# Another order of columns in the moving operand and the result of the large matmuls

## The chip, the core and the metric

The kernel runs on one core of one Trainium2 chip. The metric is the device time in microseconds of one execution; the runs shown have a median of 3166.25 us. The profiled execution was recorded by the hardware profiler, and its span goes from the first to the last instruction.

## The reference

Two transformer blocks, one after the other, over 256 tokens of width 2048, all in float32. The first mixes an HGRN2 recurrence, dilated window attention and a convolution; the second an mLSTM in chunks and differential attention. Each ends in a feed-forward layer. Cut to what the change touches:

```python
# first block
h = rms_norm(x, mix_norm_pre) * (1 + sc1) + sh1
a_q, a_f, a_i, a_g, b_q, b_k, b_v, c_a, c_g = split_cols(h @ w_in, IN_SPLITS)
gates = sigmoid(h @ w_gate + b_gate)              # 2048 x 6144
merged = gates[0] * (ya @ w_a_out) + gates[1] * (yb @ w_b_out) + gates[2] * (yc @ w_c_out)
x = x + g1 * rms_norm(merged @ w_o, mix_norm_post)
h = rms_norm(x, mlp_norm_pre) * (1 + sc2) + sh2
x = x + g2 * rms_norm(square(relu(h @ w_up)) @ w_down, mlp_norm_post)   # 8192 wide
# second block
p_lat, p_ctx = modulate(rmsnorm(x)) @ w_in_2, modulate(rmsnorm(ctx)) @ w_in_2
...                                               # mLSTM and attention over p_lat, p_ctx
x = x + ga1 * rmsnorm(y_lat, g_post_mix)
x = x + ga2 * rmsnorm(conv_ffn(h_lat, w_up_2, conv_ffn_w, conv_ffn_b, w_down_2), g_post_ffn)  # 2 x 5632 wide
```

## The kernel before, in words

Activations lie with their features on the 128 partitions and the 256 tokens along the partition. A weight matrix is cut into blocks of 2048 rows by 128 columns, laid out as `[128, 16, 128]`; these blocks are the `stream` in HBM, 1 MB each. `SECTIONS` writes their order out by hand: a "G" is a block for a matrix product, an "A" a block of the modulation weights, which VectorE multiplies and sums (`ada_column`, L1755 to L1763). SyncE loads the stream in this order into the four slots of `raw`, each as soon as the block before it in its slot is `taken`.

Precision comes from a split. A number is kept as a rounded high part and a low part, both of type float32r. ScalarE writes the high part of a weight block to `parts[:, b % 2, 0]` (`split_high`, L540), VectorE the low part to `parts[:, b % 2, 1]` (`split_low`, L1782). Activations are split in the same way. The products are high times high, high times low and low times high, so a block of 16 row tiles takes 48 matmuls of 256 columns, and each matmul has a weight load of its own.

Most blocks go through `product`, with pieces made by `features`: first, for each of the 16 row tiles k, the high weights against the high and the low part of the activations (L1041, 32 matmuls), then the low weights against the high part (L1050, 16). `gemm_T` does this for sections `a_f`, `a_q`, `b_k`, `b_q`, `a_g`, the first nine blocks of `gate`, the gates in `merge`, `w_o`, most of `up1` and `up2`, `m_q` and `d_q`. The `down` sections use `gemm_parts`, where the high and low parts of the activations lie side by side (`both`, 512 columns): 16 matmuls of 512 columns (L1077; 11 in `down2`) and as many of 256 columns (L1080), and VectorE adds the halves of the result. Others are made without these two: `branches`, `gate_chunk`, `gemm_two`, `gemm_tokens` (the weights are the moving operand there, in two runs of 128 columns), `features_wide` (512 columns in two runs, from `op_hw`, in `m_k` and `d_k`), and the work within the attention and recurrence stages.

SBUF is allocated by hand. All activation operands are regions of one arena that start at multiples of 512 bytes from one another; `parts` lies behind it, and L191 puts a gap of 16 floats (64 bytes) ahead of it:

```python
raw = sb("raw", [P, SLOTS, KT, P])
sb("parts_gap", [P, 16])
parts = sb("parts", [P, 2, 2, KT, P], F32R)
```

The feed-forward layers go in four quarters: `up1_0`, `down1_0`, `up1_1` and so on; `up2_q` and `down2_q` likewise. The row of stages in time is that of `SECTIONS`. TensorE waits for `hi_ready` (the high part of the block), for `bank_read` (the PSUM bank is free again) and, before the low part, for `taken`. There are two buffers of `parts` and four PSUM banks for results, so a block's split can run at most two blocks ahead.

Of the kernel before, what the change touches and what calls it, by code (L numbers as in the profile page):

```python
# [14 lines left out]
S = 256  # L15
D = 2048
KT = D // P
SLOTS = 4
EARLY_SLOTS, N_EARLY = 8, 48
EPS = 1e-6  # L20
TINY = 1e-30
# [46 lines left out]
def gb(name, i=0):  # L68

    return FIRST[name][1] + i  # L70
# [81 lines left out]
def two_blocks_kernel(nc, stream, x_t, ctx_t, vec_d, const_d, lvl_mask_d, ident_d, rel_bias, c_rows, scratch, x_keep, out_t):  # L152
    with ExitStack() as ctx:
        def sb(name, shape, dt=F32):
            return ctx.enter_context(nc.sbuf_tensor("sb_" + name, shape, dt))
# [33 lines left out]
        arena = sb("arena", [P, ARENA])  # L189
# [3 lines that stand above are left out]
# [172 lines left out]
        def use(n):  # L365

            if n < N_EARLY:
                return n % EARLY_SLOTS, n // EARLY_SLOTS
            return n % SLOTS, N_EARLY // EARLY_SLOTS + (n - N_EARLY) // SLOTS

        def slot_of(slot):

            return raw[:, slot] if slot < SLOTS else early_slots[slot - SLOTS]

        def kt_of(b):
            if b < KT:
                return 2 * C_TILES
            return UP2 if any(gb(f"down2_{q}") <= b < gb(f"down2_{q}") + 16 for q in range(QUARTER)) else KT
# [5 lines left out]
        def scores_bank(unit, c):  # L384

            return (M if unit % 2 == 0 else G)[c]
# [26 lines left out]
        def bank(b):  # L413
            return G[BANK[b]]
# [30 lines left out]
        @block.sync  # L445
        def _(sp):
            kts = [KT] * N_STREAM
            for b, n in enumerate(G_AT):
                kts[n] = kt_of(b)
            context_at = A_AT[127] + SLOTS  # L450

            for n in range(N_STREAM):
                slot, uses = use(n)
                if uses:
                    sp.wait_ge(taken[slot], uses)
                sp.dma_start(slot_of(slot)[:, 0:kts[n], :], stream[n][:, 0:kts[n], :]).then_inc(loaded[slot], 16)
                if n == context_at:
                    sp.wait_ge(x_ready, 5)
                    sp.dma_start(hfc, ctx_t).then_inc(cx_in, 16)
            for c, (k0, k1) in enumerate(CHUNKS):  # L460
                sp.wait_ge(x_ready, 15 + c + 1)
                sp.dma_start(out_t[:, k0:k1, :], xT[:, k0:k1, :]).then_inc(stored, 16)
            sp.wait_ge(stored, 80)
# [16 lines left out]
        def _(act):  # L480
# [50 lines left out]
            def split_high(b):  # L531

                if b >= len(G_AT):
                    return
                slot, uses = use(G_AT[b])
                kt = kt_of(b)
                act.wait_ge(loaded[slot], 16 * (uses + 1))
                if b >= 2:
                    act.wait_ge(hi_used, b - 1)
                act.activation(parts[:, b % 2, 0, 0:kt, :], slot_of(slot)[:, 0:kt, :], ACT.Copy).then_inc(hi_ready, 1)  # L540
# [478 lines left out]
        def _(pe):  # L1019
# [38 lines left out]

            def features(out, op, k0=0, k1=KT, cols=slice(0, S), kw=0):

                return (out, True, [(lambda w, x, k=k: (w[:, kw + k - k0, :], x), op[:, 0, k, cols], op[:, 1, k, cols])
                                    for k in range(k0, k1)])

            def gemm_T(b, op, it=0, dn=0, cols=slice(0, S), kt=KT, waits={}):
                product(b, [features(bank(b)[:, 0:cols.stop - cols.start], op, 0, kt, cols)], it, dn, waits=waits)

            def gemm_parts(b, op, it=0, kt=KT, waits={}):


                slot, uses = use(G_AT[b + it * 4])  # L1070
                pe.wait_ge(hi_ready, b + 1 + it * 4)
                pe.wait_ge(bank_read[BANK[b]], NTH[b] + it)
                for k in range(kt):
                    if k in waits:
                        pe.wait_ge(*waits[k])
                    both = op[:, :, k, :].rearrange("p a s -> p (a s)")
                    pe.matmul(bank(b)[:, :], parts[:, b % 2, 0, k, :], both, start=(k == 0), stop=False, skip_group_check=True)  # L1077
                pe.wait_ge(taken[slot], uses + 1)
                for k in range(kt):
                    ins = pe.matmul(bank(b)[:, 0:S], parts[:, b % 2, 1, k, :], op[:, 0, k, :], start=False, stop=(k == kt - 1),  # L1080
                                    skip_group_check=True)
                    if k == 0:
                        ins.then_inc(hi_used, 1)
                ins.then_inc(block_done, 1)

            def down_round(section, op, it, r, kt=KT, waits={}):
                for j in range(4):
                    gemm_parts(gb(section) + 4 * r + j, op, it, kt, waits if r == j == 0 else {})
# [94 lines left out]
            def ada(a, rows=M[2]):  # L1183


                slot, uses = use(A_AT[a])
                pe.wait_ge(loaded[slot], 16 * (uses + 1))
                for k in range(KT):
                    g = k % 4
                    ins = pe.matmul(rows[32 * g:32 * g + 32, 0:P], cpad[:, k, 32:64], slot_of(slot)[:, k, :],  # L1190
                                    start=(k < 4), stop=(k >= KT - 4), skip_group_check=True)
                ins.then_inc(taken[slot], 1)
# [41 lines left out]
            for n in range(4):  # L1234
                ins = pe.matmul(G[n][:, :], ones[0:1, :], c1_early[0:1, n * 512:(n + 1) * 512], start=True, stop=True)
# [26 lines left out]
            def head_row(h, src):  # L1262


                g, j = divmod(h, 2)
                return pe.matmul(M[0][32 * g:32 * g + 32, 0:S], head_sum[:, 31 - j:63 - j], src, start=(j == 0), stop=(j == 1))
# [48 lines left out]
            for n in range(BESIDE_LEVELS):  # L1315
# [19 lines left out]
                if s in (36, 37):  # L1335
                    for h in (0, 2, 4, 1, 3, 5) if s == 36 else (6, 7):
                        pe.wait_ge(o_sq, h // 2 + 1)
                        ins = head_row(h, fP[:, h, :])
# [34 lines left out]
            for u in range(10):  # L1373
                if u < 8:
                    T, slot = u // 4, u % 4
                    w = P * (T + 1)
                    if u >= 1:
                        pe.wait_ge(qk_read, u)
                    for g in range(3):
                        h = 4 * g + slot  # L1380
                        po = 64 * (h % 2)
                        out = M[0][:, g * S:g * S + w] if g < 2 else M[1][:, 0:w]
                        ins = pe.matmul(out, bq[po:po + 64, h // 2, T * P:(T + 1) * P], bk[po:po + 64, h // 2, 0:w],
                                        start=True, stop=True)
# [5 lines left out]
                if 1 <= u < 9:  # L1390
                    e, T = (u - 1) % 2, (u - 1) // 4
# [3 lines left out]
                    for i, (g, st) in enumerate((g, st) for g in range(3) for st in range(T + 1)):  # L1395
                        ins = pe.matmul(M[2 + i // 4][:, (i % 4) * P:(i % 4 + 1) * P], blog[e][:, g, st * P:(st + 1) * P],
                                        bdg[e], start=True, stop=True)
# [3 lines left out]
                if u >= 2:  # L1401
                    T, slot, e = (u - 2) // 4, (u - 2) % 4, (u - 2) % 2
# [5 lines left out]
                    for i, (g, st) in enumerate(chunk):  # L1408
                        hc = (4 * g + slot) * 64
                        ins = pe.matmul(G[3][po:po + 64, 0:P], bv[:, st, hc:hc + 64], bpt[e][:, i, :],  # L1410
                                        start=(i == 0), stop=(i == len(chunk) - 1))
# [19 lines left out]
            for t in range(EARLY_ROUNDS, 16):  # L1431
                b = gb("merge") + 4 * (t - EARLY_ROUNDS)
# [28 lines left out]
            for k in range(KT):  # L1461
                gemm_parts(gb("down1_3", k), opU1, waits=waits if k == 0 else {})
                if k == 3:
                    norm_folded(sqc, 3)
# [11 lines left out]
            for i in range(2):  # L1476
                b = gb("m_k", i)
# [28 lines left out]
            for d in range(2):  # L1506
                for t in range(2):
                    at = 64 + d * 16 + t * 8
                    ins = pe.matmul(M[1][:, at:at + 8], floor_rows[0:8, d, t * P:(t + 1) * P], ident[0:8, 0:8], start=True, stop=True)
# [102 lines left out]
            for i in range(0, 8, 2):  # L1612
# [6 lines left out]
                for c in range(i, i + 2):  # L1619
                    if c >= 2:  # L1620
                        pe.wait_ge(rope_done, c - 1)
                    for j in range(2):
                        src = dq[:, 2 * c + j, :] if c < 4 else dk[:, 2 * (c - 4) + j, S:512]
                        ins = pe.matmul(M[c % 2][:, j * S:(j + 1) * S], rtab[:, 0:P], src, start=True, stop=True)
# [37 lines left out]
            for u in range(19):  # L1662
                if u < 16:
# [3 lines left out]
                    for c in range(2):  # L1667
                        ins = pe.matmul(scores_bank(u, c)[:, :], dq[64 * c:64 * c + 64, h, T * P:(T + 1) * P], dk[64 * c:64 * c + 64, h, :],
                                        start=True, stop=True)
# [4 lines left out]
                if 2 <= u < 18:  # L1674
                    e = u % 2
# [3 lines left out]
                    for t in range(4):  # L1679
                        ins = pe.transpose(M[2][:, t * P:(t + 1) * P], dpd[e][:, t * P:(t + 1) * P], ident[:, :])  # L1680
# [3 lines left out]
                if u >= 3:  # L1684
                    h, e = (u - 3) // 2, (u - 3) % 2
# [4 lines left out]
                    for t in range(4):  # L1690
                        ins = pe.matmul(M[3][:, 0:P], dv[:, t, h * P:(h + 1) * P], dPT[e][:, t, :], start=(t == 0),
                                        stop=(t == 3))
# [43 lines left out]
            for k in range(KT):  # L1736
                gemm_parts(gb("down2_3", k), opU2, kt=UP2, waits=waits if k == 0 else {})
# [4 lines left out]
        def _(dve):  # L1742
# [23 lines left out]
            def ada_made(a_end):  # L1766


                for a in range(a_end - SLOTS, a_end):
                    slot, uses = use(A_AT[a])  # L1770
# [809 lines left out]
```

## Time and profile before

| | |
|---|---|
| median of the runs | 3166.25 us (3160.32 to 3176.34) |
| profiled execution | 3166.26 us, its span 3164.5 us |
| mean granted TensorE clock | 0.996 |
| busy: TensorE, its weight loads, VectorE, ScalarE | 3095.9, 2919.9, 2369.1, 1336.6 us |
| read from HBM | 712.41 MB |

Busy time is the union of an engine's instructions. A matmul's length includes its way through the array and overlaps the next one's, so the distance from one start to the next is the time that a matmul takes in a row of many; a busy time divided by a count comes near it. A weight load (PEld) overlaps the matmuls. A window's row has its length, then the busy time (and in brackets the count of the instructions that lie in it or across its edges) of TensorE, weight loads, VectorE, ScalarE and GpSimd, then the granted TensorE clock, the busy share of the DMA engines and GB/s.

### The profile page before, as it was taken

How to read it: one execution, taken by the hardware profiler on the slowest of the kernel's cores; microseconds unless marked ns; L12 is line 12 of the kernel's file. 1: busy time of each engine (PE TensorE's matmuls, PEld its weight loads, DVE VectorE, ACT ScalarE, POOL GpSimd, SP SyncE). 2: the span in 40 equal slices, each digit the busy share in tenths (PEclk: the TensorE clock that was granted, in tenths of full speed). 3: DMA queues.
4: the chain of work that ended last, by engine and by line, in shares of the span. 5: the costliest groups of instructions: out<-in, count | busy, mean ns of one | idle time of the engine just before them, and what ended most of it. 6: DMA issues, size and time to landing. Idle time of an engine off the chain costs nothing.

```text
span 3164.5 us, 55394 instructions
## 1 busy us (share of the span) xinstructions
PE 3095.9 (98%) x23974; PEld 2919.9 (92%) x23974; DVE 2369.1 (75%) x2843; ACT 1336.6 (42%) x1459; POOL 1.8 (0%) x10
## 2 busy tenths in 40 slices
PE   7899999999999999999999999999999999999998
PEld 6899999999999999998988999989889989999996
DVE  5799876688887789899978766644667666777766
ACT  3333344444444443333464334521465444344444
POOL 0000000000000000000000000000000000000000
PEclk9999999999999999999999999999999999999999
DMA  9864444488894887777855763354343575665643
GB/s 403 329 222 161 161 160 153 173 351 342 331 360 161 305 312 272 268 266 283 300 189 202 277 245 149 142 209 168 120 145 135 182 261 187 225 224 209 244 171 136
DMA packets 106417, 722.62 MB, mean 228 GB/s; under 512 B 11677, under 2 KB 15389, under 8 KB 27197
## 3 DMA queue, kind: packets, MB, share of 16 engines
q1 hardware_dynamic: 100368, 703.64, 60.0%
q10 hardware_dynamic: 5806, 15.43, 1.6%
q8 instruction: 190, 3.11, 0.4%
q14 instruction: 53, 0.43, 0.0%
HBM read 712.41 MB, written 6.55 MB: 227 GB/s over the span
## 4 chain that ended last, share of the span: by engine, by line
PE 89%; DVE 6%; DMA 2%; ACT 1%; issue 1%; ACTq 0%; DVEq 0%
PE gemm L1041 39%; PE gemm L1050 19%; PE gemm L1077 12%; PE gemm L1080 6%; DVE sb_parts L1782 1%; DMA sb_raw<-stream 1%; PE mix L1041 1%; PE mix L1292 1%; PE mix L1572 1%; ACT sb_parts L540 1%; DMA sb_arena<-x_t 1%; DVE sb_arena L1837 1%; PE gemm L1208 1%; PE mix L1050 1%; DVE sb_arena L1893 1%
## 5 line engine op out<-in xcount | busy, mean ns | idle before, releaser
L540 ACT ACTIVATE sb_parts<-sb_raw 128x2048 fp32r<-128x2048 f32 (+2 forms) x489 | 902.4, 1848 | 1471.5 <-PE gemm L1050 947.4
L1782 DVE TENSOR_TENSOR sb_parts<-sb_raw,sb_parts 128x2048 fp32r<-128x2048 f32 (+2 forms) x489 | 1071.9, 2194 | 301.8 <-PE gemm L1050 152.5
L1041 PE MATMUL gemm<-op_h,sb_parts 128*128 128x256 f32 x7232 | 873.6, 279 | 2.1 <-ACT sb_parts L540 1.7
L1041 PEld LDWEIGHTS gemm<-op_h,sb_parts 128*128 128x128 f32 x7232 | 850.3, 188 | 3.7 <-ACT sb_parts L540 2.3
L1050 PE MATMUL gemm<-op_h,sb_parts 128*128 128x256 f32 x3616 | 454.0, 278 | 0.1
L1050 PEld LDWEIGHTS gemm<-op_h,sb_parts 128*128 128x128 f32 x3616 | 433.7, 188 | 0.3 <-DVE sb_parts L1782 0.3
L1077 PE MATMUL gemm<-op_up,sb_parts 128*128 128x512 f32 x1728 | 424.7, 395 | 2.9 <-DVE op_up L2411 2.9
L1077 PEld LDWEIGHTS gemm<-op_up,sb_parts 128*128 128x128 f32 x1728 | 315.5, 188 | 70.6 <-DVE op_up L2411 4.6
L1080 PEld LDWEIGHTS gemm<-op_up,sb_parts 128*128 128x128 f32 x1728 | 217.2, 188 | 11.4
L1763 DVE CUSTOM_DVE_ANT_0 sb_raw<-sb_raw,sb_arena,sb_vec 128x2048 f32<-128x2048 f32 x96 | 224.4, 2348 | 1.5 <-DMA sb_raw<-stream 0.4
L1080 PE MATMUL gemm<-op_up,sb_parts 128*128 128x256 f32 x1728 | 219.0, 278 | 0.0
L1041 PE MATMUL gemm<-op_hw,sb_parts 128*128 128x256 f32 (+1 forms) x992 | 175.9, 335 | 0.3 <-ACT sb_parts L540 0.3
L1041 PEld LDWEIGHTS gemm<-op_hw,sb_parts 128*128 128x128 f32 x992 | 149.7, 188 | 22.3 <-ACT sb_parts L540 0.5
L1755 DVE CUSTOM_DVE_ANT_0 sb_raw<-sb_raw,sb_arena,sb_vec 128x2048 f32<-128x2048 f32 x64 | 149.8, 2345 | 0.0
L2402 DVE SCALAR_TENSOR_TENSOR sb_arena<-gemm,sb_vec,sb_arena 128x255 f32<-128x255 f32 x88 | 42.5, 483 | 136.5 <-ACT sb_arena L992 136.5
L1041 PE MATMUL gemm<-sb_parts,op_hw 128*128 128x256 f32 x1024 | 123.7, 282 | 0.4 <-ACT sb_parts L540 0.4
L1041 PEld LDWEIGHTS gemm<-sb_parts,op_hw 128*128 128x128 f32 x1024 | 122.4, 190 | 1.6 <-issue 0.8
L1050 PE MATMUL gemm<-op_hw,sb_parts 128*128 128x256 f32 (+1 forms) x496 | 90.3, 334 | 0.0
L1050 PEld LDWEIGHTS gemm<-op_hw,sb_parts 128*128 128x128 f32 x496 | 75.5, 188 | 11.0
L1817 DVE TENSOR_TENSOR sb_arena<-gemm,sb_arena 128x256 f32<-128x256 f32 x96 | 40.5, 422 | 53.3 <-PE gemm L1080 53.1
L1762 DVE CUSTOM_DVE_ANT_0 sb_arena<-sb_raw,sb_arena,sb_vec 128x2048 f32<-128x2048 f32 x32 | 75.1, 2345 | 0.0
L1208 PE MATMUL gemm<-op_h,sb_parts 128*128 128x256 f32 x384 | 57.8, 288 | 16.9 <-DVE sb_parts L1782 13.4
(360 smaller groups left out, 3342.2 us busy)
## 6 DMA issues: line engine op xcount, KB each, us to landing
sb_raw<-stream SPq DMA_DIRECT2D x597, 1024.0 KB, 5.0
sb_raw<-stream SPq DMA_DIRECT2D x64, 704.0 KB, 4.1
sb_arena<-stream SPq DMA_DIRECT2D x14, 1024.0 KB, 8.4
sb_arena<-stream SPq DMA_DIRECT2D x10, 768.0 KB, 8.0
sb_raw<-stream SPq DMA_DIRECT2D x6, 768.0 KB, 7.7
sb_arena<-c_rows ACTq DMA_DIRECT2D x3, 1024.0 KB, 7.0
bias_rows<-sb_arena ACTq DMA_DIRECT2D x1, 2304.0 KB
sb_arena<-x_t ACTq DMA_DIRECT2D x4, 512.0 KB, 18.9
```

Source lines behind the costliest of these rows:

```text
L540: act.activation(parts[:, b % 2, 0, 0:kt, :], slot_of(slot)[:, 0:kt, :], ACT.Copy).then_inc(hi_ready, 1)
L1041: ins = pe.matmul(out, l, r, start=(opens and i == 0 and x is xh), stop=False, skip_group_check=True)
L1050: ins = pe.matmul(out, l, r, start=False, stop=(i == len(terms) - 1), skip_group_check=True)
L1077: pe.matmul(bank(b)[:, :], parts[:, b % 2, 0, k, :], both, start=(k == 0), stop=False, skip_group_check=True)
L1080: ins = pe.matmul(bank(b)[:, 0:S], parts[:, b % 2, 1, k, :], op[:, 0, k, :], start=False, stop=(k == kt - 1), skip_group_check=True)
L1208: ins = pe.matmul(out[:, i * S:(i + 1) * S], w, opH[:, p, k, :], start=(k == i == part == p == 0), stop=(k == KT - 1 and part == 1), skip_ ...
L1755: dve.tensor_tensor_reduce(w, w, c1_row, 1.0, v("b_ada", a), ALU.mult, ALU.add, mod1[:, a:a + 1])\
L1762: step(dve.tensor_tensor_reduce(products, w, cctx_row, 1.0, v("b_mod", a), ALU.mult, ALU.add, mod2[:, 1, a:a + 1]))
L1763: dve.tensor_tensor_reduce(w, w, c2_row, 1.0, v("b_mod", a), ALU.mult, ALU.add, mod2[:, 0, a:a + 1])\
L1782: dve.tensor_tensor(parts[:, b % 2, 1, 0:kt, :], slot_of(slot)[:, 0:kt, :], parts[:, b % 2, 0, 0:kt, :].bitcast(F32), ALU.subtract).then_i ...
L1817: step(dve.tensor_tensor(acc, bank(b)[:, 0:S], acc, ALU.add))
L2402: step(dve.scalar_tensor_tensor(y[:, 1:S], src[:, 0:S - 1], w0, y[:, 1:S], ALU.mult, ALU.add))
```

## The change

A helper `by_line` turns the last dimension of an operand into three: groups, two halves, and 16 elements (64 bytes of float32). Walking through it in order gives line 0, then the line half an operand further, then line 1, and so on: 0, 8, 1, 9 for 256 columns, 0, 16, 1, 17 for 512. The helper is put around the moving operand and around the output in PSUM of the matmuls in `features` and `gemm_parts`, so each result column lands where it did. The stationary operand is read as before. Everything else is the same.

```diff
--- before.py
+++ after.py
@@ -16,6 +16,7 @@
 D = 2048
 KT = D // P
 SLOTS = 4
+LINE = 16
 EARLY_SLOTS, N_EARLY = 8, 48
 EPS = 1e-6
 TINY = 1e-30
@@ -371,6 +372,11 @@
         def slot_of(slot):
 
             return raw[:, slot] if slot < SLOTS else early_slots[slot - SLOTS]
+
+        def by_line(t):
+
+
+            return t.rearrange("p (b g e) -> p g b e", b=2, e=LINE)
 
         def kt_of(b):
             if b < KT:
@@ -1058,8 +1064,8 @@
 
             def features(out, op, k0=0, k1=KT, cols=slice(0, S), kw=0):
 
-                return (out, True, [(lambda w, x, k=k: (w[:, kw + k - k0, :], x), op[:, 0, k, cols], op[:, 1, k, cols])
-                                    for k in range(k0, k1)])
+                return (by_line(out), True, [(lambda w, x, k=k: (w[:, kw + k - k0, :], x), by_line(op[:, 0, k, cols]), by_line(op[:, 1, k, cols]))
+                                             for k in range(k0, k1)])
 
             def gemm_T(b, op, it=0, dn=0, cols=slice(0, S), kt=KT, waits={}):
                 product(b, [features(bank(b)[:, 0:cols.stop - cols.start], op, 0, kt, cols)], it, dn, waits=waits)
@@ -1074,10 +1080,10 @@
                     if k in waits:
                         pe.wait_ge(*waits[k])
                     both = op[:, :, k, :].rearrange("p a s -> p (a s)")
-                    pe.matmul(bank(b)[:, :], parts[:, b % 2, 0, k, :], both, start=(k == 0), stop=False, skip_group_check=True)
+                    pe.matmul(by_line(bank(b)[:, :]), parts[:, b % 2, 0, k, :], by_line(both), start=(k == 0), stop=False, skip_group_check=True)
                 pe.wait_ge(taken[slot], uses + 1)
                 for k in range(kt):
-                    ins = pe.matmul(bank(b)[:, 0:S], parts[:, b % 2, 1, k, :], op[:, 0, k, :], start=False, stop=(k == kt - 1),
+                    ins = pe.matmul(by_line(bank(b)[:, 0:S]), parts[:, b % 2, 1, k, :], by_line(op[:, 0, k, :]), start=False, stop=(k == kt - 1),
                                     skip_group_check=True)
                     if k == 0:
                         ins.then_inc(hi_used, 1)
```

## Rows read from the trace of the kernel before

**Rows 1.** The page, part 1: busy us, share, instructions.

```profile
PE 3095.9 (98%) x23974; PEld 2919.9 (92%) x23974; DVE 2369.1 (75%) x2843; ACT 1336.6 (42%) x1459; POOL 1.8 (0%) x10
```

**Rows 2.** The page, part 4: the chain that ended last.

```profile
PE 89%; DVE 6%; DMA 2%; ACT 1%; issue 1%; ACTq 0%; DVEq 0%
PE gemm L1041 39%; PE gemm L1050 19%; PE gemm L1077 12%; PE gemm L1080 6%; DVE sb_parts L1782 1%; DMA sb_raw<-stream 1%; PE mix L1041 1%; PE mix L1292 1%; PE mix L1572 1%; ACT sb_parts L540 1%; DMA sb_arena<-x_t 1%; DVE sb_arena L1837 1%; PE gemm L1208 1%; PE mix L1050 1%; DVE sb_arena L1893 1%
```

**Rows 3.** Timeline of TensorE in down1_1: start us, length us, line, count.

```profile
1255.98 3.89 PE L1077 MATMUL gemm<-op_up,sb_parts 128*128 128x512 f32 x16
1259.70 1.98 PE L1080 MATMUL gemm<-op_up,sb_parts 128*128 128x256 f32 x16
1261.52 1.79 PE L1077 MATMUL gemm<-op_up,sb_parts 128*128 128x512 f32 x7
```

**Rows 4.** Windows in up2_0, up2_1 and up2_2.

```profile
2430.00:2530.00 100.00, 100.00 (x885) 100.00 (x884) 70.12 (x83) 46.29 (x46) 0.00 (x0) 1.00 0.54 190
2600.00:2700.00 100.00, 100.00 (x852) 100.00 (x851) 67.41 (x80) 44.40 (x44) 0.00 (x0) 1.00 0.51 180
2800.00:2900.00 100.00, 100.00 (x881) 99.87 (x880) 67.77 (x83) 46.88 (x48) 0.00 (x0) 1.00 0.53 185
```

**Rows 5.** Timeline of TensorE in a_i (tokens), m_k and d_k blocks.

```profile
250.57 3.93 PE L1050 MATMUL gemm<-sb_parts,op_h 128*128 128x256 f32 x32
1715.60 7.63 PE L1041 MATMUL gemm<-op_hw,sb_parts 128*128 128x512 f32 x32
2072.29 7.63 PE L1041 MATMUL gemm<-op_hw,sb_parts 128*128 128x512 f32 x32
```

**Rows 6.** Windows: start, a_f/a_q, down1_0, down1_1, down1_2, d_q/d_k.

```profile
0.00:140.00 140.00, 112.79 (x1162) 97.64 (x1162) 87.90 (x125) 48.85 (x67) 1.77 (x10) 0.99 0.94 388
140.00:231.00 91.00, 90.69 (x768) 90.52 (x768) 83.42 (x138) 40.01 (x42) 0.00 (x0) 1.00 0.69 218
1056.00:1136.00 80.00, 80.00 (x463) 69.68 (x463) 67.27 (x56) 29.94 (x28) 0.00 (x0) 1.00 0.95 354
1239.00:1320.00 81.00, 81.00 (x480) 70.96 (x479) 78.54 (x74) 27.85 (x15) 0.00 (x0) 1.00 0.80 293
1403.00:1500.00 97.00, 97.00 (x587) 85.53 (x586) 94.38 (x89) 34.86 (x20) 0.00 (x0) 1.00 0.81 292
2020.00:2160.00 140.00, 140.00 (x818) 121.95 (x818) 66.47 (x56) 42.42 (x36) 0.00 (x0) 1.00 0.53 199
```

**Rows 7.** Groups by line and shape: busy us, mean ns | idle before.

```profile
L1041 PE MATMUL gemm<-op_h,sb_parts 128*128 128x256 f32 x7232 | 873.6, 279 | 2.1 <-ACT sb_parts L540 1.7 <-DVE sb_arena L1929 0.5
L1050 PE MATMUL gemm<-op_h,sb_parts 128*128 128x256 f32 x3616 | 454.0, 278 | 0.1
L1077 PE MATMUL gemm<-op_up,sb_parts 128*128 128x512 f32 x1728 | 424.7, 395 | 2.9 <-DVE op_up L2411 2.9
L1080 PE MATMUL gemm<-op_up,sb_parts 128*128 128x256 f32 x1728 | 219.0, 278 | 0.0
L1041 PE MATMUL gemm<-op_merged,sb_parts 128*128 128x256 f32 x512 | 61.2, 277 | 1.8 <-ACT sb_parts L540 1.7
L1041 PE MATMUL gemm<-op_hw,sb_parts 128*128 128x256 f32 x512 | 61.4, 278 | 0.0
L1050 PE MATMUL gemm<-op_hw,sb_parts 128*128 128x256 f32 x256 | 31.9, 277 | 0.0
L1050 PE MATMUL gemm<-op_merged,sb_parts 128*128 128x256 f32 x256 | 31.6, 276 | 0.0
L1041 PEld LDWEIGHTS gemm<-op_h,sb_parts 128*128 128x128 f32 x7232 | 850.3, 188 | 3.7 <-ACT sb_parts L540 2.3 <-issue 0.8 <-DVE sb_arena L1929 0.6
```

**Rows 8.** Matmuls of plain fp32: timeline in the mLSTM stage, and one group.

```profile
2003.85 1.02 PE L1557 MATMUL gemm<-sb_arena 128*128 128x256 f32 x4
2004.71 1.73 PE L1572 MATMUL mix<-sb_arena 128*128 128x129 f32 x14
...
L1680 PE MATMUL mix<-sb_ident,sb_arena 128*128 128x128 f32 x64 | 9.6, 273 | 0.0
```

## The prediction

> **What bounds the kernel now.** I read the page's busy line first: TensorE is busy 3095.9 us of a span of 3164.5, VectorE 75%, ScalarE 42% [rows 1]. The chain that ended last is 89% TensorE, three quarters of the span in four source lines [rows 2]: L1041 and L1050 in `product`, L1077 and L1080 in `gemm_parts`. The change rewrites the operands of all matmuls that `gemm_parts` and `features` make. So the question is whether TensorE spends more time on such a matmul than its columns need, and whether another order of the columns gives that back.
>
> For that I turn to starts, because the mean length of one (279 ns) overlaps its neighbours. In the timeline of a `down1` block [rows 3] 16 matmuls of 512 columns start at 1255.98 and the next line at 1259.70: 3.72 us / 16 = 232.7 ns each. The 16 of 256 columns that follow take (1261.52 - 1259.70) / 16 = 113.8 ns. [...]
>
> The windows in three of the four `up2` quarters are of one loop on the same buffers, and yet there are two levels [rows 4]: 100 us hold 885 matmuls in `up2_0` and 852 in `up2_1` (two or three of each lie across an edge), so 113.3 ns against 117.7 ns; the third quarter is at the first level again. Clock, VectorE and DMA shares are nearly alike. A fixed limit of the array would give one level. Two levels of the same code look like two streams whose relative phase, once fallen into, stays. Who is the second stream? Not VectorE or the DMA: wide matmuls take (7.63 - 0.40) / 31 = 233.2 ns in `m_k` and as much in `d_k`, where VectorE is busy 47% of the time, and 232.7 in `down1_1`, where it is 97% [rows 3, 5, 6]. [...]
>
> What is the floor? [...] The new order reads two lines half an operand apart, then the next two. [...] I take 109.2 and 215.7 ns as the new starts.
>
> **Part by part.** Nothing is added or removed as an instruction: same matmuls, loads, semaphores, DMAs. Only the address patterns change.
>
> (a) What there is now. A group's busy time holds, for each block, a tail of one length less one spacing (0.163 us; 0.162 for the wide ones), which has to come off [rows 7]. `op_h` L1041: (873.6 - 226 x 0.163) / 7232 = 115.7 ns. L1050: (454.0 - 36.8) / 3616 = 115.4. L1077: (424.7 - 128 x 0.162) / 1728 = 233.8. L1080: (219.0 - 20.9) / 1728 = 114.7. `op_merged`: 16 blocks, 114.4 and 113.3. `op_hw` of 256 columns: 16 blocks, 114.8 and 114.4 ns.
>
> (b) What each gives down to 109.2 or 215.7: 7232 x 6.5 = 47.0; 3616 x 6.2 = 22.4; 1728 x 18.1 = 31.3; 1728 x 5.5 = 9.5; merged 2.7 + 1.0; hw 2.9 + 1.3. Sum 118.1 us. The first matmuls of blocks wait a little for ScalarE or VectorE, which is in these means and does not go; I take 5 us off: 113 us. Ends for this term: zero if the order does not matter, 118 if no such wait is in it.
>
> (c) Who is late next. Per `down1` block TensorE would save 16 x 17.0 + 16 x 4.6 = 0.346 us of 5.54, to 5.19. VectorE is busy 78.54 of 81 us and 94.38 of 97 us in `down1_1` and `down1_2` [rows 6], which at 14.6 and 17.5 blocks of 5.54 us is 5.37 and 5.39 us a block. There it takes over: 0.18 x 14.6 + 0.20 x 17.5 = 6 us of the gain are lost. In `down1_0` the DMA engines are busy 95% at 354 GB/s; the faster block asks for 378, and the start of the kernel shows 388 at 94%, so 0 to 4 us, I take 2. In `a_f` and `a_q` VectorE has 83.42 us in 91 [rows 6], 5.21 a block against 48 x 109.2 = 5.24: just covered; it costs nothing. ScalarE has room everywhere. If VectorE's cover went altogether, these stages would stay as long as now, 14 us more.
>
> (d) The address jumps. A 256-column matmul gets 16 runs of 16 columns where it had one. The nearest rows: the wide matmuls on `op_hw` read two runs that lie far apart, at 233.2 ns, and `op_up` one run, at 232.7; the token matmuls read two runs of `parts` with 117.7 ns ((3.93 - 0.28) / 31), the upper of the two levels [rows 3, 5]. So one jump of the read costs 0 to 0.5 ns, and I take 0. [...]
>
> Sum: 113 - 6 - 2 = 105 us. The profiled execution took 3166.26 us, 1.8 around its span of 3164.5, and the median of the runs is 3166.25, so the two are the same: 3166 - 105 = 3061 us.
>
> [...]
>
> **The rivals.** [...]
>
> *The order does not matter.* [...] The levels would then fall anew by chance: all upper is 14,112 x 2.4 = +34, all lower -30, more likely a third of that. 3155 to 3175, middle 3166.
>
> *Writing in runs costs more than reading them saves.* The place is PSUM, where every matmul here adds to what stands there; it decides from 6.2 / 16 = 0.39 ns a run, where the gain of a 256-column matmul is gone. [...] For it: no matmul of this kernel writes a broken pattern, so nothing shows that it is free. Against: the read jumps cost nothing. [...]
>
> **How the numbers follow.** Freed 0.50 (3045 to 3085, 3061), partly freed 0.16 (3110), no matter 0.15 (3166), slower writes 0.19 (3284). The range leaves out the last: 3045 to 3180. What a measurement can tell from no change is about 0.5%, 16 us. Faster: 0.50 + 0.16 + 0.01 = 0.67; the same 0.13; slower 0.19 + 0.01 = 0.20.
>
> **What would show it.** In the changed kernel's timeline a `down1` block's L1077 matmuls should start 216 ns apart and L1080's 109 (now 233 and 114), and the four `up2` quarters should have one level, some 915 matmuls in 100 us. `m_k`, `m_v`, `d_k`, `d_v` are untouched and stay at 233 and 113 or 118. VectorE should be near 100% in `down1_1` and `down1_2`, with TensorE waiting there. The forecast is wrong if L1077 stays at 233 (second rival), if both levels survive lower down (first), or if matmuls grow with their number of runs (third); it is wrong in size if VectorE or the DMA queue holds more stages than the three named.

## The result, and the profile after

The changed kernel takes 3248.23 us in the median (3246.84 to 3249.41), against 3171.3 us for the kernel before in the runs beside it (3160.32 to 3181.42; the 3166.25 us that the forecast started from is the median of three of these four). The ratio is 1.0243, with a 95% interval of 1.0205 to 1.0281: 2.4% slower, where 3% faster was forecast. The span of the profiled execution went from 3164.5 to 3247.6 us. The page's first part, to be held against [rows 1]:

```profile
PE 3181.7 (98%) x23974; PEld 2999.0 (92%) x23974; DVE 2370.8 (73%) x2843; ACT 1337.0 (41%) x1459; POOL 1.8 (0%) x10
```

TensorE's busy time rose by 85.8 us, more than the span's 83.1. VectorE's and ScalarE's did not move. The timeline of a `down1_1` block says where it went (start, length of the row, line, count):

```profile
1282.45 4.00 PE L1083 MATMUL gemm<-op_up,sb_parts 128*128 128x512 f32 x16
1286.29 2.08 PE L1086 MATMUL gemm<-op_up,sb_parts 128*128 128x256 f32 x16
1288.21 4.00 PE L1083 MATMUL gemm<-op_up,sb_parts 128*128 128x512 f32 x16
```

(1286.29 - 1282.45) / 16 = 240.0 ns for 512 columns, and (1288.21 - 1286.29) / 16 = 120.0 ns for 256. In [rows 3] they were 232.7 and 113.8. The windows that answer to [rows 4], in `up2_0` and `up2_1` of the changed kernel:

```profile
2490.00:2590.00 100.00, 100.00 (x836) 100.00 (x835) 66.02 (x82) 43.28 (x45) 0.00 (x0) 1.00 0.51 178
2680.00:2780.00 100.00, 100.00 (x836) 100.00 (x835) 65.28 (x79) 44.43 (x45) 0.00 (x0) 1.00 0.50 173
```

836 matmuls in either, less two or three at the edges: 120.0 ns. The granted clock is 1.00 there as it was before. The two levels of before, 113.3 and 117.7 ns, are gone, as the prediction said, but into one above both. The groups by line, against [rows 7] (L1047 was L1041, L1056 was L1050, L1083 was L1077, L1086 was L1080):

```profile
L1047 PE MATMUL gemm<-op_h,sb_parts 128*128 128x256 f32 x7232 | 907.6, 284 | 1.2 <-ACT sb_parts L546 0.7 <-DVE sb_arena L1935 0.5
L1056 PE MATMUL gemm<-op_h,sb_parts 128*128 128x256 f32 x3616 | 470.8, 283 | 0.0
L1083 PE MATMUL gemm<-op_up,sb_parts 128*128 128x512 f32 x1728 | 436.8, 403 | 2.6 <-DVE op_up L2417 2.6
L1086 PE MATMUL gemm<-op_up,sb_parts 128*128 128x256 f32 x1728 | 228.2, 283 | 0.0
```

With the tails taken off as in the prediction these are 120.4, 120.0, 240.8 and 120.0 ns, so 34.0 + 16.8 + 12.1 + 9.2 us more than before. `op_merged` and `op_hw` of 256 columns bring 9 more: 81 of the 83 us. The untouched forms stayed where they were (`op_hw` of 512 columns: 114.5 us busy in both).

The numbers are round. 240.0 is twice 120.0: 7.5 ns for each run of 16 columns, whatever the matmul's length. That was the first reading; the experiments below do not bear it out for other run lengths. They had to say whether that is paid for reading or for writing, for the broken order or for the pairing of lines, and what it has to do with the weight load.

### The profile page after: what moved, and what is told of

Same layout as the page of the kernel before. It is cut to its first block, busy times and chain, and to the rows that moved or that the text cites. A ratio compares the mean times of both kernels' runs of the same rounds, so it can differ in the third digit from the quotient of the medians.

```text
span 3247.6 us, 55394 instructions
## 1 busy us (share of the span) xinstructions
PE 3181.7 (98%) x23974; PEld 2999.0 (92%) x23974; DVE 2370.8 (73%) x2843; ACT 1337.0 (41%) x1459; POOL 1.8 (0%) x10
## 4 chain that ended last, share of the span: by engine, by line
PE 90%; DVE 6%; DMA 2%; ACT 1%; issue 1%; ACTq 0%; DVEq 0%
PE gemm L1047 40%; PE gemm L1056 19%; PE gemm L1083 13%; PE gemm L1086 6%; PE mix L1047 1%; DVE sb_parts L1788 1%; DMA sb_raw<-stream 1%; PE mix L1298 1%; PE mix L1578 1%; DMA sb_arena<-x_t 1%; PE gemm L1214 1%; ACT sb_parts L546 1%; DVE sb_arena L1843 1%; PE mix L1056 1%; PE mix L1157 1%
## 5 line engine op out<-in xcount | busy, mean ns | idle before, releaser
L1047 PE MATMUL gemm<-op_h,sb_parts 128*128 128x256 f32 x7232 | 907.6, 284 | 1.2 <-ACT sb_parts L546 0.7
L1047 PEld LDWEIGHTS gemm<-op_h,sb_parts 128*128 128x128 f32 x7232 | 883.7, 190 | 2.6 <-ACT sb_parts L546 1.1
L1056 PE MATMUL gemm<-op_h,sb_parts 128*128 128x256 f32 x3616 | 470.8, 283 | 0.0
L1056 PEld LDWEIGHTS gemm<-op_h,sb_parts 128*128 128x128 f32 x3616 | 449.9, 190 | 0.1
L1083 PE MATMUL gemm<-op_up,sb_parts 128*128 128x512 f32 x1728 | 436.8, 403 | 2.6 <-DVE op_up L2417 2.6
L1083 PEld LDWEIGHTS gemm<-op_up,sb_parts 128*128 128x128 f32 x1728 | 320.9, 191 | 76.5 <-DVE op_up L2417 4.4
L1086 PEld LDWEIGHTS gemm<-op_up,sb_parts 128*128 128x128 f32 x1728 | 225.4, 190 | 12.4
L1086 PE MATMUL gemm<-op_up,sb_parts 128*128 128x256 f32 x1728 | 228.2, 283 | 0.0
L1769 DVE CUSTOM_DVE_ANT_0 sb_raw<-sb_raw,sb_arena,sb_vec 128x2048 f32<-128x2048 f32 x96 | 224.3, 2348 | 1.1
L1047 PE MATMUL gemm<-op_hw,sb_parts 128*128 128x256 f32 (+1 forms) x992 | 178.7, 337 | 0.4 <-ACT sb_parts L546 0.4
L1047 PEld LDWEIGHTS gemm<-op_hw,sb_parts 128*128 128x128 f32 x992 | 152.4, 189 | 22.4 <-ACT sb_parts L546 0.6
L1047 PE MATMUL gemm<-sb_parts,op_hw 128*128 128x256 f32 x1024 | 124.3, 282 | 0.7 <-ACT sb_parts L546 0.7
L1047 PEld LDWEIGHTS gemm<-sb_parts,op_hw 128*128 128x128 f32 x1024 | 122.9, 190 | 1.9 <-ACT sb_parts L546 0.9
L1823 DVE TENSOR_TENSOR sb_arena<-gemm,sb_arena 128x256 f32<-128x256 f32 x96 | 40.5, 422 | 74.3 <-PE gemm L1086 74.3
L1056 PE MATMUL gemm<-op_hw,sb_parts 128*128 128x256 f32 (+1 forms) x496 | 91.8, 337 | 0.0
L1056 PEld LDWEIGHTS gemm<-op_hw,sb_parts 128*128 128x128 f32 x496 | 76.8, 189 | 11.0
L2147 DVE TENSOR_TENSOR sb_arena<-sb_arena 128x256 f32<-128x256 f32 x64 | 27.1, 424 | 72.4 <-ACT sb_arena L797 70.9
```

The source lines that it names most:

```text
L1047: ins = pe.matmul(out, l, r, start=(opens and i == 0 and x is xh), stop=False, skip_group_check=True)
L1056: ins = pe.matmul(out, l, r, start=False, stop=(i == len(terms) - 1), skip_group_check=True)
L1083: pe.matmul(by_line(bank(b)[:, :]), parts[:, b % 2, 0, k, :], by_line(both), start=(k == 0), stop=False, skip_group_check=True)
L1086: ins = pe.matmul(by_line(bank(b)[:, 0:S]), parts[:, b % 2, 1, k, :], by_line(op[:, 0, k, :]), start=False, stop=(k == kt - 1), skip_group ...
L1769: dve.tensor_tensor_reduce(w, w, c2_row, 1.0, v("b_mod", a), ALU.mult, ALU.add, mod2[:, 0, a:a + 1])\
L1823: step(dve.tensor_tensor(acc, bank(b)[:, 0:S], acc, ALU.add))
```

## The experiments

**One side alone.** Two kernels have the change on one side only.

```diff
# read_only: moving operand by_line, output plain
-                return (by_line(out), True, [(lambda w, x, k=k: ..., by_line(op[:, 0, k, cols]), by_line(op[:, 1, k, cols]))
+                return (out, True, [(lambda w, x, k=k: ..., by_line(op[:, 0, k, cols]), by_line(op[:, 1, k, cols]))
# write_only: output by_line, moving operand plain
+                return (by_line(out), True, [(lambda w, x, k=k: ..., op[:, 0, k, cols], op[:, 1, k, cols])
# and both the same way in gemm_parts
```

Both leave their results' tokens in another order than the reference has; the matmuls are the same in number and size. Theory R is that the read in pieces costs, theory W that the write to PSUM does.

> The change on the moving operand alone; the output keeps its plain order, so the tokens of the results land in another order than the reference has. Theory R: 120.0 and 240.0 ns a matmul as in the changed kernel, 3248 us. Theory W: the reads cost nothing, 109 to 118 ns and 216 to 233, 3060 to 3166 us. If both must be broken to cost: as before, 3166.

> The change on the PSUM output alone; the moving operand is read in plain order, so the tokens of the results land in another order than the reference has. Theory W: 120.0 and 240.0 ns a matmul, 3248 us. Theory R: 113.3 or 117.8 and 233 ns, 3166 us, level changes apart (3135 to 3200).

Reading alone: 3248.48 us, ratio 1.0272 (1.0245 to 1.0300). Writing alone: 3163.37 us, ratio 0.9997 (0.9980 to 1.0014). The rows of L1047 and L1083 of reading alone are those of the changed kernel, printed above, to the last digit (907.6 and 436.8 us). Writing alone has:

```profile
L1047 PE MATMUL gemm<-op_h,sb_parts 128*128 128x256 f32 x7232 | 865.1, 277 | 1.3 <-ACT sb_parts L546 0.7 <-DVE sb_arena L1935 0.5
```

Its wide matmuls are busy 424.7 us, as before. Its 865.1 us are 8.5 below the 873.6 of before: at (865.1 - 36.8) / 7232 = 114.5 ns on average, more of its rows stood at the lower of the two levels. The whole price is the read's; the write in runs of 64 bytes has none (a ratio of 0.9997).

**Many forms in one kernel.** The kernel `probe1` is the one before with rows of 44 matmuls behind its last norm, one form to a line (cut to one of the loops). The probes ran once each, and their rows are compared within one execution:

```diff
             norm_sum(sq2, 1, KT)
+            for n in range(44):                    # one such loop for each form
+                w, x = probe_of(n)                 # weights of tile k, op_up of tile k, 512 columns
+                pe.matmul(acc[:, 0:256], w, runs(x[:, 0:256], 16), start=(n == 0), stop=False, ...)
```

> The kernel before with 31 rows of 44 extra matmuls each on TensorE behind its last norm (float32r parts of the weights and up2 operands, into one free PSUM bank, not used), one source line per form. [...] Theory P (the pairing 0, 8, 1, 9 lands both reads on one place): odd lines behind even lines cost nothing, only runs16 does. [...] Theory Phase (two levels come from how moving read and weight load stand to one another): plain reads that begin 16, 32, 64, 128 columns further differ from each other by up to 5 ns; a fixed limit expects them all alike.

Its timeline behind the last norm. A form's spacing is the next row's start less its own, over its count. L1763 is written in runs of 16, L1766 read and written in 16, L1769 in 32, L1772 in 64, L1775 read in 8, L1778 written in 8, L1781 read even lines before odd ones, L1784 written so; L1790 is 512 columns plain, L1793 read in 16, L1796 written in 16; L1805 plain fp32 (two records for each matmul), L1808 that read in 16; L1817, L1820 and L1823 plain, begun 16, 32 and 64 columns further; L1838 384 columns, L1841 320.

```profile
3159.11 5.35 PE L1763 MATMUL mix<-op_up,sb_parts 128*128 128x256 f32 x44
3164.29 5.45 PE L1766 MATMUL mix<-op_up,sb_parts 128*128 128x256 f32 x44
3169.57 5.39 PE L1769 MATMUL mix<-op_up,sb_parts 128*128 128x256 f32 x44
3174.80 5.17 PE L1772 MATMUL mix<-op_up,sb_parts 128*128 128x256 f32 x44
3179.81 5.58 PE L1775 MATMUL mix<-op_up,sb_parts 128*128 128x256 f32 x44
3185.24 5.17 PE L1778 MATMUL mix<-op_up,sb_parts 128*128 128x256 f32 x44
3190.24 5.50 PE L1781 MATMUL mix<-op_up,sb_parts 128*128 128x256 f32 x44
3195.58 5.16 PE L1784 MATMUL mix<-op_up,sb_parts 128*128 128x256 f32 x44
...
3205.85 10.41 PE L1790 MATMUL mix<-op_up,sb_parts 128*128 128x512 f32 x44
3216.11 10.72 PE L1793 MATMUL mix<-op_up,sb_parts 128*128 128x512 f32 x44
3226.67 10.43 PE L1796 MATMUL mix<-op_up,sb_parts 128*128 128x512 f32 x44
3236.94 5.16 PE L1799 MATMUL mix<-op_up,sb_parts 128*128 128x256 f32 x44
...
3246.92 19.15 PE L1805 MATMUL mix<-op_up,sb_parts 128*128 128x256 f32 x88
3265.91 19.16 PE L1808 MATMUL mix<-op_up,sb_parts 128*128 128x256 f32 x88
3284.91 19.16 PE L1811 MATMUL mix<-op_up,sb_parts 128*128 128x256 f32 x88
...
3322.71 5.62 PE L1817 MATMUL mix<-op_up,sb_parts 128*128 128x256 f32 x44
3328.16 5.35 PE L1820 MATMUL mix<-op_up,sb_parts 128*128 128x256 f32 x44
3333.35 5.16 PE L1823 MATMUL mix<-op_up,sb_parts 128*128 128x256 f32 x44
3338.34 5.15 PE L1826 MATMUL mix<-op_up,sb_parts 128*128 128x256 f32 x44
...
3358.62 7.84 PE L1838 MATMUL mix<-op_up,sb_parts 128*128 128x384 f32 x44
3366.30 6.62 PE L1841 MATMUL mix<-op_up,sb_parts 128*128 128x320 f32 x44
3372.75 5.35 PE L1844 MATMUL mix<-op_up,sb_parts 128*128 128x256 f32 x44
```

- Runs of 16 read and written: (3169.57 - 3164.29) / 44 = 120.0 ns; of 32: 118.9; of 64: 113.9, as plain. Read in 8: 123.4, so 32 runs cost 10.1 ns above the lower level where 16 cost 6.7: the price does not go by the number of runs. Written in 16: 117.7, in 8: 113.6, the two levels of plain. Even lines before odd: 121.4. So it is not the pairing 0, 8: each float32r read tried with pieces of 32 columns or less pays, and with pieces of 64 nothing is paid.
- 512 columns: plain 233.2, read in 16 240.0, written in 16 233.4 ns.
- Plain fp32: 18.99 us / 88 = 215.8 ns with one run and with sixteen: there the order is free. The float32r row of 128 columns beside these (L1835, with a load of 128 columns for each) stands (3358.62 - 3353.75) / 44 = 110.7 ns apart, and the plain fp32 ones of L1680 in [rows 8] stand 109.7 apart within a group of four. 128 columns more cost 60.0 ns in longer float32r matmuls (the item after next), so the 110.7 are not the price of the columns alone, and such a short row says little of the moving read.
- Begun 16 columns (one line) further: (3328.16 - 3322.71) / 44 = 123.9 with the change-over in it; from the fourth on they stand 119.8 apart. 32 further: 118.0, 64 further: 113.4. Same loads, same order, and up to 7 ns between them.
- 384 columns: (3366.30 - 3358.62) / 44 = 174.5, in the steady part 173.3. So 128 columns more cost 60.0 ns from 256 to 384 and again from there to 512, which is 7.5 ns for each line of 64 bytes, the very price that the broken order in runs of 16 has.
- 320 columns: (3372.75 - 3366.30) / 44 = 146.6 ns.

One fit to these sizes: in the plain order, too, a line costs 7.5 ns, and 6.7 ns come off once in each matmul. Then 16 x 7.5 - 6.7 = 113.3, 24 x 7.5 - 6.7 = 173.3 and 32 x 7.5 - 6.7 = 233.3 ns, and the broken order, from which nothing comes off, costs 6.7 ns more at either width, less where the upper level held. The fit fails at 320 columns, where it gives 143.3 ns against 146.6, and it says nothing of runs of 32 and 8. So the sizes are measured, but the mechanism behind them is not shown.

**What the price hangs on.** `probe2` has more forms, 36 matmuls each.

> The kernel before with more rows of extra matmuls behind its last norm, results not used. [...] Theory Level: the level is set by the distance in lines between moving operand and weights modulo 8; from 0 keeps whichever level it is put into, from 64 always 113.3, and moving the weights by +64 does the same. Rival: the levels are chance, and each offset shows either after either disturbance.

Timeline. L1902 has weights of 32 columns and 256 plain, L1905 the same with 512, L1908 with 256 read in runs of 16; L1911 weights of 64 columns; L1929 is 512 read in runs of 32, L1932 in 64, L1935 in 128; L1938 reads one line 16 times over; L1941 each of 8 lines twice, line by line; L1944 those 8 lines with each column twice running; L1947 every second column of 512; L1950 runs of 4; L1953 bf16, plain, L1956 the same read in runs of 32.

```profile
3324.20 4.25 PE L1902 MATMUL mix<-op_up,sb_parts 128*32 128x256 f32 x36
3328.28 8.48 PE L1905 MATMUL mix<-op_up,sb_parts 128*32 128x512 f32 x36
3336.60 4.48 PE L1908 MATMUL mix<-op_up,sb_parts 128*32 128x256 f32 x36
3340.92 4.26 PE L1911 MATMUL mix<-op_up,sb_parts 128*64 128x256 f32 x36
...
3374.64 8.68 PE L1929 MATMUL mix<-op_up,sb_parts 128*128 128x512 f32 x36
3383.16 8.56 PE L1932 MATMUL mix<-op_up,sb_parts 128*128 128x512 f32 x36
3391.56 8.56 PE L1935 MATMUL mix<-op_up,sb_parts 128*128 128x512 f32 x36
3399.96 4.48 PE L1938 MATMUL mix<-op_up,sb_parts 128*128 128x256 f32 x36
3404.28 4.49 PE L1941 MATMUL mix<-op_up,sb_parts 128*128 128x256 f32 x36
3408.60 4.18 PE L1944 MATMUL mix<-op_up,sb_parts 128*128 128x256 f32 x36
3412.62 8.43 PE L1947 MATMUL mix<-op_up,sb_parts 128*128 128x256 f32 x36
3420.87 4.74 PE L1950 MATMUL mix<-op_up,sb_parts 128*128 128x256 f32 x36
3425.45 4.11 PE L1953 MATMUL mix<-sb_ones 128*128 128x256 bf16 x36
3429.39 4.09 PE L1956 MATMUL mix<-sb_ones 128*128 128x256 bf16 x36
```

With a quarter of the weights plain matmuls are at (3328.28 - 3324.20) / 36 = 113.3 and the broken ones at 120.0, as with all of them: had the broken read collided with the weight load, as my theory had it, its price should have shrunk with the load, and it did not. No row goes without any load, and no broken read began at another distance from the weights, so a part of the load in it is not excluded. With a quarter of the weights 512 plain columns cost (3336.60 - 3328.28) / 36 = 231.1 ns, so 2.2 of the 233.3 ns go with the load's length. Reading one line over and over costs (3404.28 - 3399.96) / 36 = 120.0 as well; what costs is to start a piece of 16 columns, new line or not. The same eight lines with each column read twice running (L1944) take 111.7 ns, bf16 (3429.39 - 3425.45) / 36 = 109.4. The bf16 row read in runs of 32 columns, again 64 bytes (L1956), is no longer than the plain one: 4.09 against 4.11 us for 36. So the pace in columns is not what makes a broken read pay: bf16 takes its 256 columns faster than float32r does. In bytes a partition the two forms whose order is free are slower, by an estimate from these spacings: plain fp32 has 1024 in the 215.8 ns of a record and bf16 512 in 109.4, 4.7 a ns, and float32r 1024 in 113.3, 9.0. Whether that decides was not tested. In 512 columns runs of 32 cost 236.7 and of 64 and 128 233.3. Every second column costs 229.2 ns for 32 lines in 256 columns, 7.2 ns a line, and runs of 4 cost (3425.45 - 3420.87) / 36 = 127.2.

The weight load does matter for the level. Rows begun 0, 64 and 128 columns further settle at 113.4 ns, 16 and 80 at 120.0, 32 and 96 at 117.8, 48 and 112 at 118.6 or 118.8, after either disturbance; moving the weights by 16, 32, 48, 64 gives 118.8, 117.8, 119.7, 113.4. The distance between the two operands counts modulo 64 columns, 256 bytes (not modulo 512 bytes, as I had it). A plain read begun 16 columns further costs the same 120.0 ns as a broken one; whether the two have one cause was not tested.

**Four lines further.** By the theory of that time `parts_gap` of 80 floats should have given the lower level everywhere.

```diff
-        sb("parts_gap", [P, 16])
+        sb("parts_gap", [P, 80])
```

> The kernel before (plain order) with the gap ahead of parts of 80 floats in place of 16, so the weights lie four lines of 64 bytes further against the moving operands. Theory Level: all changed-form matmuls of 256 columns fall into the lower level, 113.3 ns, in all stages: 14112 x 2.1 = 30 us less, 3135 us. Rival (levels by chance): both levels remain, 3150 to 3175 us.

It ran at 3165.34 us, ratio 0.9995 (0.9985 to 1.0006), and both levels remained (`op_h` in L1041 had (871.3 - 36.8) / 7232 = 115.4 ns a matmul, between them). This fits a period of 64 columns, since 80 and 16 are then the same place. My expectation missed.

**Part of the change, and other run lengths.** `parts_only` has the change in `gemm_parts` alone; `line32` and `line64` are the changed kernel with `LINE = 32` and `64`.

> The change in gemm_parts alone (the down sections), features as before. If the price is per matmul and adds up: L1077 233.8 to 240.0 and L1080 114.7 to 120.0, 1728 x (6.2 + 5.3) = 20 us more than before, 3183 us, and the other 56 to 60 us of the change belong to features. If the down sections wait on VectorE in any case: less than 10 us more.

> The changed kernel with runs of 32 columns (two lines) in place of 16. The extra rows had 118.8 ns for 256 columns in such runs and 236.7 for 512: 14112 x 3.4 + 1728 x 3.0 = 53 us more than before, 3220 us, between 3248 (runs of 16) and before (runs of 64). [...]

> The changed kernel with runs of 64 columns in place of 16 (LINE = 64): 4 runs for 256 columns, 8 for 512. [...]

| kernel | median us | ratio (95%) |
|---|---|---|
| parts_only | 3184.04 | 1.0059 (1.0046 to 1.0073) |
| line32 | 3226.38 | 1.0157 (1.0139 to 1.0176) |
| line64 | 3165.62 | 1.0003 (0.9988 to 1.0019) |

The `op_h` group of `line32`:

```profile
L1047 PE MATMUL gemm<-op_h,sb_parts 128*128 128x256 f32 x7232 | 898.6, 282 | 1.2 <-ACT sb_parts L546 0.7 <-DVE sb_arena L1935 0.5
```

`parts_only` is 17 us above before (20 expected), so the price adds up over the lines that have it. `line32` is 51 us above (53 expected from the extra rows, (898.6 - 226 x 0.163) / 7232 = 119.2 ns a matmul). Half the runs cost nearly as much, 119.2 ns against 120.4 in the changed kernel, so here too the price does not go by their number. `line64` is as before: neither a gain nor a loss.

**Can the levels or the wide matmuls be had cheaper?** The upper level costs 4.5 ns a matmul. `probe3` looked for what ends it.

> The kernel before with rows of extra matmuls behind its last norm, results not used. Each row first puts the array into the upper level of plain matmuls of 256 columns (117.8 ns) by runs of 16 and then reads begun 32 columns further, then has one or two odd matmuls, then 36 plain ones. Theory Level (the level is a phase that a matmul of another length or line distance resets): after nothing the plain ones stay at 117.8; after one matmul begun 16 columns further, or one plain fp32, they fall to 113.3. Rival (it needs a long disturbance): all stay at 117.8. 512 columns as two matmuls of 256 with the same weights: 226.6 ns a pair in the lower level, 235.6 in the upper, against 233.3 for one.

Plain rows after the upper level and one matmul whose columns are read twice each (L1878), and after one with weights 16 columns further (L1890):

```profile
3255.89 4.40 PE L1878 MATMUL mix<-op_up,sb_parts 128*128 128x256 f32 x36
3260.13 2.56 PE L1881 MATMUL mix<-op_up,sb_parts 128*128 128x256 f32 x20
...
3265.00 4.24 PE L1890 MATMUL mix<-op_up,sb_parts 128*128 128x256 f32 x36
3269.08 2.72 PE L1893 MATMUL mix<-op_up,sb_parts 128*128 128x512 f32 x11
```

(3260.13 - 3255.89) / 36 = 117.8 and (3269.08 - 3265.00) / 36 = 113.3. One matmul of the second kind ends the upper level there, and so do one read begun 16 columns further, one plain of 16 columns, two of 128 and two of 512; one fp32, one of 64, of 128 or of 512 columns do not. The pairs that stand for a wide matmul (two of 256 with the same weights) took 226.7 ns behind the lower level (66 matmuls at 113.3) and 235.6 behind the upper (66 at 117.8), as expected. Then in the real stages:

```diff
+            def level_down(b, op, it=0):            # ahead of about 80 blocks
+                ...                                 # the block's own waits
+                shifted = parts[:, b % 2, 0].rearrange("p k b -> p (k b)")[:, 16:16 + P]
+                pe.matmul(bank(b)[:, 0:S], shifted, op[:, 0, 0, :], start=True, stop=False, skip_group_check=True)
```

```diff
 # halves, and reset_halves
-                    pe.matmul(bank(b)[:, :], parts[:, b % 2, 0, k, :], both, start=(k == 0), ...)
+                    for a in range(2):
+                        pe.matmul(bank(b)[:, a * S:(a + 1) * S], parts[:, b % 2, 0, k, :], op[:, a, k, :], start=(k == a == 0), ...)
```

> The kernel before (plain order), but each matmul of 512 columns in gemm_parts is two of 256 with the same weights. [...] If the pair falls into the upper level, 235.6: 4 us more, 3170 us.

> The kernel before (plain order) with one more matmul ahead of about 80 blocks that go through gemm_T, into the block's own bank before its first matmul clears it, with weights read 16 columns further on: in the extra rows one such matmul brought the array from the upper level (117.8 ns) to the lower (113.3). Theory Level: the op_h, op_merged and op_hw matmuls of 256 columns are all at 113.3; 12384 x 2.1 = 26 us less, 80 x 0.118 = 9 us more, 3150 us. Rival (something in the stages puts them back at once): the share of the upper level stays near two fifths, 3175 us.

> The same and each matmul of 512 columns in gemm_parts as two of 256, with the extra matmul ahead of each four blocks of the down sections too (about 25 more). Theory Level: another 1728 x 6.7 + 1728 x 1.4 less and 3 us more, so 11 us below the run of reset, 3139 us. Rival (the halves gain nothing where VectorE or the DMA is late next): as reset, 3150.

`halves`: 3172.95 us, ratio 1.0002 (0.9975 to 1.0030). `reset`: 3180.98 us, 1.0016 (1.0005 to 1.0027). `reset_halves`: 3169.61 us, 0.9999 (0.9977 to 1.0021). No gain shows in the medians; the 3150 and 3139 that were hoped for with the reset did not come, nor did the 3155 of `halves` (pairs of 226.7 ns in place of 233.3, 1728 x 6.7 = 12 us less), and `reset` is slightly slower. In the profiled execution of `halves` the halved matmuls were busy 417.2 us against 424.7 for the wide ones in the profile of the kernel before. A gain of 7.5 us there lies within the interval of that run, about 9 us either way, so it is neither shown nor excluded. The timeline of `reset` in `up2_1` has the inserted matmul at L1069:

```profile
2646.83 0.28 PE L1069 MATMUL gemm<-op_h,sb_parts 128*128 128x256 f32 x1
2646.95 3.93 PE L1041 MATMUL gemm<-op_h,sb_parts 128*128 128x256 f32 x32
2650.72 2.05 PE L1050 MATMUL gemm<-op_h,sb_parts 128*128 128x256 f32 x16
```

Behind it the row still goes at (2650.72 - 2646.95) / 32 = 117.8 ns, where such a matmul ended the upper level in `probe3`. (There it came behind reads begun 32 columns further, here behind plain ones.) It was so 12 of the 13 times that an inserted matmul came without idle time behind 256-column rows at the upper level.

What sets the level in the real stages can be read in part from the kernel before. In `down2`, where a block has 11 wide matmuls, each such row turns the level over (a row of 11 lasts 1.46 us at the upper level and 1.42 at the lower; timeline of TensorE from 2545.2 to 2551 us):

```profile
2545.30 1.46 PE L1080 MATMUL gemm<-op_up,sb_parts 128*128 128x256 f32 x11
2546.60 2.73 PE L1077 MATMUL gemm<-op_up,sb_parts 128*128 128x512 f32 x11
2549.16 1.42 PE L1080 MATMUL gemm<-op_up,sb_parts 128*128 128x256 f32 x11
```

That holds for 60 of 60 such rows in this trace and as many in each of `gap80` and the three probes, up to their last norm. The rows of 16 wide matmuls in `down1` never raised it: 58 of 59 rows in this trace found and left the lower level, and one went from the upper to the lower. Two rows of 256 columns in L1041 and L1050 that follow each other without idle time had the same level in all but 3 of the 2363 cases of these five traces in which each row stood at one of the two levels; where 150 ns or more lay between two starts, it changed in 6 of 20. What an idle time does to it stays open.

The time of an execution goes with the levels. `probe1` was at the end of `down2` at 3146.6 us, with 114.5 ns for a mean `op_h` matmul; `probe2` at 3162.4, with 115.6. The 10,848 of them make an estimated 12 of these 16 us. The executions of `reset_halves` lie between 3152.11 and 3187.39 us, and the profiled one, the fastest, was in the lower level nearly throughout:

```profile
L1041 PE MATMUL gemm<-op_h,sb_parts 128*128 128x256 f32 x7232 | 858.1, 276 | 0.0
L1088 PE MATMUL gemm<-op_up,sb_parts 128*128 128x256 f32 x3456 | 416.0, 277 | 2.6 <-DVE op_up L2423 2.6
```

(858.1 - 36.8) / 7232 = 113.6 ns. No version here was clearly faster than the kernel before.

## Why the prediction was wrong

**The step that failed** is the floor: "I take 109.2 and 215.7 ns as the new starts." Both were my estimate, and no run shows them for these matmuls. The rows of plain fp32 [rows 8] stand near them ((2004.71 - 2003.85) / 4 = 215 ns for 256 columns in L1557, 109.7 for 128 in L1680), but in `probe1` the order makes no difference at all to plain fp32 (215.8 ns in one run and in sixteen), so it says nothing of float32r. In float32r no order of the 256 or 512 columns with full weights came below the plain one's 113.3 and 233.3. The new order makes 120.0 and 240.0. So term (b), 113 us of gain, came out as 81 us of loss.

**The price of the jumps** (part d) was the second half of it. Reads were taken to be free because the rows with one jump were. But their runs are 128 and 256 columns long, and runs of 64 and 128 are free (233.3 ns for 512 columns, as plain); the count of jumps was the wrong measure and their length the right one. The read's true price comes to 6.7 ns a matmul above the lower level and 2.2 above the upper, and 6.7 for a wide one. The third rival's 3284 us rests on a price for each run of the write to PSUM that was my estimate; no run shows it, and the write was free (a ratio of 0.9997). Its time was nearer to the result than anything else in the forecast, with the wrong place. The 3110 us of *partly freed* rests on an estimate as well, of what part would be gained; no run here shows such a part, and the changed kernel gained none.

**The levels.** That two levels of one loop look like two streams whose phase stays fits the runs as far as they go: the distance between the moving operand and the weights sets the spacing (113.4 to 120.0), and what ran before sets the level (113.3 or 117.8). That the new order would free what this costs was wrong: it replaced both levels by a slower pace, 120.0 ns, the same with a quarter, half and all of the weights.

**The second rival**, that the order does not matter, was the better reading: from 256 columns to 384 and to 512 each line costs 7.5 ns in the plain order, and no order freed it. It lacked that a broken order can be slower than the plain one.

**The terms.** The sum itself was sound in form: 15,840 matmuls times a difference, and the path takes nearly all of it (81 of 83 us). Its sign was wrong with the floor. The cover (part c) was never put to the test, since TensorE became slower: the untested 8 us.

**The chances.** The third rival had 0.19 and lay outside the range of 3045 to 3180. Given that no float32r row had short runs, either side was an extrapolation, and half the weight on the favourable one was too much.

## What to carry to other kernels

Before an access pattern is broken into pieces, ask how long the pieces are and of what type the operand is: here, in float32r, pieces of 64 columns were free (113.9 ns, as plain) and pieces of 16 cost 6% of a 256-column matmul (113.3 to 120.0 ns), while in pieces of 64 bytes writes to PSUM (a ratio of 0.9997), plain fp32 (215.8 ns either way) and bf16 (4.09 against 4.11 us for 36) did not mind. A floor has to be taken from rows of the same type and width. What looks like waste in a steady state may be a limit that no order lifts; a row of a few dozen matmuls behind the kernel's end measures each form within one run.

## What the runs showed that was not expected

- A float32r matmul of N columns in plain order costs 113.3, 173.3 and 233.3 ns at N = 256, 384 and 512: 60.0 ns for every 128 columns more; at 320 it is 146.6. bf16 has 109.2 ns at 256 in the steady part of its row.
- What a piece costs does not go by the pace in columns: bf16, with 109.4 ns for 256, was free in pieces of 64 bytes, and float32r, with 113.3, was not (120.0).
- The spacing depends on how far apart moving and stationary operand begin, modulo 64 columns: 113.4, 120.0, 117.8, 118.7 ns at 0, 16, 32, 48 from the present place. By these rows a gap in the allocation could decide about 6%; no whole kernel was run at 16, 32 or 48 columns from the present place.
- At the present distance there are two levels, 113.3 and 117.8 ns. A row of 256-column matmuls hands its level on to the next one if no idle time lies between; in `down2` each row of 11 wide matmuls turns it over. Which level a stage falls into differs between executions of one kernel, and the spread of 3155 to 3190 us goes with it in part.
